# A hybrid decoder layer on one core: another order of the row phase, and half of the softmax normalisation on VectorE

## The reference

```python
hn = rmsnorm(h, g_attn_norm)
z = hn @ w_in                     # q: 8 heads of 64, k and v: 2 heads of 64, u: 4 groups of 128
q, k = rmsnorm per head           # gains g_q, g_k
logits = q k^T / 8 + bias[bucket(distance)]     # a window of 128 keys, blocks of 128 queries
m = max(max(logits), sink)
probs = exp(logits - m) / (sum(exp(logits - m)) + exp(sink - m))
a = probs @ v
pooled_g = trailing mean of u_g over 2, 4, 8, 16 tokens, minus u_g
m_g = (pooled_g @ w_pool_g) * pool_scale_g
h = h + concat(a, m) @ w_out
h = h + (silu(hn @ w_gate) * (hn @ w_up)) @ w_down
h = h + sigmoid(rmsnorm(h) @ w_ple_gate) * (p @ w_ple_proj)
```

## Time and profile before

| | us |
|---|---|
| median of 3 runs | 2166.16 |
| lowest, highest | 2163.57, 2167.04 |
| the profiled execution, whole | 2166.23 |
| its span, first to last instruction | 2164.3 |
| TensorE busy in the span | 2094.3 |
| VectorE busy | 1405.8 |
| ScalarE busy | 963.7 |
| GpSimd busy | 304.6 |

### The profile page before, as it was taken

How to read it: one execution, slowest core, us unless ns; L and a number is a source line. 1 busy time by engine, 2 the same in 40 slices (tenths; PEclk the granted TensorE clock), 3 DMA queues, 4 the chain that set the end, 5 groups by cost and what they waited for, 6 DMA issues and landing times.

```text
span 2164.3 us, 27230 instructions
## 1 busy us (share of the span) xinstructions
PE 2094.3 (97%) x10008; PEld 1746.6 (81%) x10008; DVE 1405.8 (65%) x1994; ACT 963.7 (45%) x1608; POOL 304.6 (14%) x448
## 2 busy tenths in 40 slices
PE   6999999999899999999999999999999999999998
PEld 5787877877777888888888888788888888888887
DVE  4566775776777556565588865685655656987653
ACT  3375575676664333333343354533333333333542
POOL 1423244152322000000000010000000000000100
PEclk9999999999999999999999999999999999999999
DMA  6431435433275232322572413842323236533143
GB/s 175 117 79 49 132 76 154 117 98 108 59 248 185 69 102 68 95 81 65 203 258 83 132 40 108 223 137 73 98 69 104 67 102 211 213 112 103 49 125 99
DMA packets 198879, 253.46 MB, mean 117 GB/s; under 512 B 14923, under 2 KB 128252, under 8 KB 197468
## 3 DMA queue, kind: packets, MB, share of 16 engines
q1 hardware_dynamic: 183888, 207.73, 32.7%
q0 software_dynamic: 12880, 42.51, 5.5%
q10 hardware_dynamic: 1980, 1.50, 0.3%
HBM read 201.88 MB, written 49.80 MB: 116 GB/s over the span
## 4 chain that ended last, share of the span: by engine, by line
PE 84%; DVE 5%; issue 4%; ACT 3%; DMA 3%; POOL 1%; SPq 0%; ACTq 0%; DVEq 0%; POOLq 0%
PE bank L2324 12%; PE bank L2328 12%; PE bank L2326 12%; PE bank L2030 7%; PE bank L2386 6%; PE bank L2387 6%; PE bank L2388 6%; PE bank L2032 6%; PE bank L2031 6%; PE bank L2056 1%; PE bank L2098 1%; ACT w_hi L872 1%; PE bank L2111 1%; DMA raw<-in_w_ple_gate 1%; PE bank L2047 1%
## 5 line engine op out<-in xcount | busy, mean ns | idle before, releaser
L2324 PE MATMUL bank<-a_hi,ring_hi 128*128 128x512 f32 x1232 | 482.3, 391 | 5.9 <-ACT u L1105 3.0
L2328 PE MATMUL bank<-a_hi,ring_lo 128*128 128x512 f32 x1232 | 481.2, 391 | 0.0
L2326 PE MATMUL bank<-a_lo,ring_hi 128*128 128x512 f32 x1232 | 481.1, 390 | 0.0
L2324 PEld LDWEIGHTS bank<-a_hi,ring_hi 128*128 128x128 f32 x1232 | 232.4, 189 | 55.4 <-ACT u L1105 3.9
L2326 PEld LDWEIGHTS bank<-a_lo,ring_hi 128*128 128x128 f32 x1232 | 232.4, 189 | 48.3
L2328 PEld LDWEIGHTS bank<-a_hi,ring_lo 128*128 128x128 f32 x1232 | 232.2, 188 | 48.4
L1348 DVE TENSOR_TENSOR w_lo<-raw,w_hi 128x1024 fp32r<-128x1024 f32 x112 | 147.5, 1317 | 175.3 <-ACT w_hi L872 174.7
L2386 PE MATMUL bank<-d_hi 128*128 128x512 f32 x616 | 240.8, 391 | 0.0
L2388 PE MATMUL bank<-d_hi,d_lo 128*128 128x512 f32 x616 | 239.8, 389 | 0.0
L2387 PE MATMUL bank<-d_lo,d_hi 128*128 128x512 f32 x616 | 239.7, 389 | 0.0
L1182 ACT ACTIVATE d_hi<-keep 128x1024 fp32r<-128x1024 f32 x132 | 139.8, 1060 | 201.5 <-PE bank L2388 184.5
(11 more groups left out here) (237 smaller groups left out, 4018.8 us busy)
## 6 DMA issues: line engine op xcount, KB each, us to landing
hidden_T<-hid POOLq DMA_DIRECT2D x88, 256.0 KB, 2.3
raws<-in_w_gate SPq DMA_DIRECT2D x84, 256.0 KB, 4.6
raws<-in_w_up SPq DMA_DIRECT2D x84, 256.0 KB, 5.3
raw<-in_w_in SPq DMA_DIRECT2D x80, 256.0 KB, 3.9
keep<-hidden_T SPq DMA_DIRECT2D x66, 256.0 KB, 3.8
raw<-in_w_out SPq DMA_DIRECT2D x64, 256.0 KB, 4.0
raw<-in_w_ple_gate SPq DMA_DIRECT2D x64, 256.0 KB, 4.1
keep<-in_w_down SPq DMA_DIRECT2D x44, 256.0 KB, 4.2
```

The source lines that it names most:

```text
L2324: mm(dst[:, :], wh[:, g, cols], a_hi[o][:, k, :], start=fresh and k == 0, stop=False, skip_group_check=True)
L2326: mm(dst[:, :], wh[:, g, cols], a_lo[o][:, k, :], start=False, stop=False, skip_group_check=True)
L2328: ins = mm(dst[:, :], wl[:, g, cols], a_hi[o][:, k, :], start=False, stop=k == 3, skip_group_check=True)
```

## The change

1. **Dense hosting.** In z1, out2 and now the beginning of out0 and out3, steps stand one to a half. Before, four halves carried two steps (half 19 of z1, and halves 5, 8 and 11 of out2).
2. **Panels of the output projection** in the order 2, 3, 0, 1 (`OUT_ORDER`): pooled channels first, attention's channels last.
3. **Pooling earlier.** Its sums, mean and rest two steps earlier. `pool_y` of tiles 0 to 2 moves from the out section into halves 16 to 18 of the z section ahead of it, in `bank0` and `bank1`. For tile 3 it moves to halves 13 to 15 of out2 and half 0 of out3, ahead of the hosted step there.
4. **Late splits on VectorE.** In an even half that hosts a step, `w_lo` is made behind the step and not ahead of it. ScalarE's `w_hi` stays ahead.
5. **Norms.** The norm-1 pieces of blocks 0 and 1 alternate between `bank7` and `bank4`. The squares of the norm-2 rows move to halves 0 to 2, their scaling to halves 3, 6, 8 and 12, and one transposed piece from half 8 to half 10.
6. **Start.** The first two `norm_hi`/`norm_lo` come around the first `split`; every later one follows one block sooner; `load_constants` moves behind them, and VectorE's work on the constants moves into half 1 of z0.
7. **Normalisation.** ScalarE normalises the first head of each unit alone; VectorE normalises the second directly behind its reciprocal (a new `tensor_scalar` of 128 x 256). TensorE's transpose waits for both.

```diff
+DENSE_Z = {h: (h - 2,) for h in range(2, 20)}
+DENSE_O = {h: (h,) for h in range(16)}
+HOST = {("z", 1): ((0, DENSE_Z),), ("o", 0): ((0, {0: (18,)}), (1, SPREAD)), ("z", 2): ((1, SPREAD_Z),),
+        ("o", 1): ((2, SPREAD),), ("z", 3): ((2, SPREAD_Z),), ("o", 2): ((3, DENSE_O),),
+        ("o", 3): ((3, {h: (h + 16,) for h in range(3)}),)}
+OUT_ORDER = (2, 3, 0, 1)
...
+POOL_Z, POOL_Z_COPY = {16: (0,), 17: (1,), 18: (2, 3)}, {17: (0,), 18: (1,), 19: (2, 3)}
+POOL_O2, POOL_O2_COPY = {13: (0,), 14: (1,), 15: (2,)}, {14: (0,), 15: (1,)}
+POOL_O3, POOL_O3_COPY = {0: (3,)}, {0: (2,), 1: (3,)}
...
             def normalise(n, c):
                 act.wait_ge(rden_done, n + 1)
-                for j in range(2):
-                    ins = nc.scalar.activation(scores[:, c, j, 0:2 * P], scores[:, c, j, 0:2 * P], ACT.Copy,
-                                               scale=rden[:, c % 2, j:j + 1])
-                ins.then_inc(pnorm, 1)
+                nc.scalar.activation(scores[:, c, 0, 0:2 * P], scores[:, c, 0, 0:2 * P], ACT.Copy,
+                                     scale=rden[:, c % 2, 0:1]).then_inc(pnorm, 1)
...
                 nc.vector.reciprocal(rden[:, i, :], row_sum[:, i, :]).then_inc(rden_done, 1)
+                dve.wait_ge(rden_done, n + 1)
+                nc.vector.tensor_scalar(out=scores[:, c, 1, 0:2 * P], in0=scores[:, c, 1, 0:2 * P],
+                                        scalar1=rden[:, i, 1:2], scalar2=None, op0=ALU.mult
+                                        ).then_inc(pnorm2, 1)
...
                 pe.wait_ge(pnorm, n + 1)
+                pe.wait_ge(pnorm2, n + 1)
...
-                    if half % 2 == 0:
+                    late = bool(hosted_steps("z", t, half))
+                    if half % 2 == 0 and not late:
                         split(Z_AT[t] + half // 2 + 1)
...
                     hosted("z", t, half)
+                    if half % 2 == 0 and late:
+                        split(Z_AT[t] + half // 2 + 1)
...
                 if b == 1:
+                    norm_hi(0, bank[4], wide_hi, 0, 0)
                     split(0)
-                    load_constants()
+                    norm_hi(1, bank[5], wide_hi, 1, 0)
...
+            load_constants()
             z_section(0)
```

More of the change, by code:

```diff
@@ L323, in mix_of, with hosted_steps, pool_bank, norm1_bank @@
             return (wide_hi, wide_lo) if s == NT - 1 else (mix_hi, mix_lo)
+        def hosted_steps(kind, t, half):
+            return [(s, k) for s, steps in HOST.get((kind, t), ()) for k in steps.get(half, ())]
+        def pool_bank(s, g):
+            return bank[7 if s == NT - 1 else g % 2]
+        def norm1_bank(b, e):
+            return bank[4 if e and b < 2 else 7]
         def h_of(t):
@@ L742, in hosted @@
             def hosted(kind, t, half):
[L743 to L746 removed]
+                for s, k in hosted_steps(kind, t, half):
+                    attention_step(s, k)
             def store_n2(t, b, e):
@@ L761, in z_section @@
                 for half in range(20):
-                    if t >= 2 and 1 <= half <= 4:
-                        powers(NORM2[t - 2], half - 1)
+                    if t >= 2:
+                        for b in N2_SQUARES_AT.get(half, ()):
+                            powers(NORM2[t - 2], b)
                     if t in (0, 3):
@@ L999, in hosted @@
                     stage_q(s, 0)
-                if (kind, t) in HOST:
-                    s, steps = HOST[kind, t]
-                    for k in steps.get(half, ()):
-                        attention_step(s, k)
+                for s, k in hosted_steps(kind, t, half):
+                    attention_step(s, k)
             def z_section(t):
@@ L1930, in out_section @@
                 for half in range(16):
-                    if half % 2 == 0 and OUT_AT[t] + half // 2 + 1 < ROW_PANELS:
+                    due = half % 2 == 0 and OUT_AT[t] + half // 2 + 1 < ROW_PANELS
+                    late = bool(hosted_steps("o", t, half))
+                    if due and not late:
                         split(OUT_AT[t] + half // 2 + 1)
-                    if half < 4:
-                        pool_y_rest(t, half)
+                    for g in {2: POOL_O2_COPY, 3: POOL_O3_COPY}.get(t, {}).get(half, ()):
+                        pool_y_rest(3, g)
                     if t < 2:
@@ L1964, in out_section @@
                     hosted("o", t, half)
+                    if due and late:
+                        split(OUT_AT[t] + half // 2 + 1)
             dve.wait_ge(gain_landed, 16)
@@ L2143, in put_off @@
                     kind, t, half = ("o", t - 2, 16) if kind == "z" else ("z", t + 1, 20)
-                if (kind, t) in HOST:
-                    s, steps = HOST[kind, t]
-                    for k in steps.get(half - 1, ()):
-                        if next_block(k):
-                            return lambda: transpose_probs(s, k)
+                for s, k in hosted_steps(kind, t, half - 1):
+                    if next_block(k):
+                        return lambda: transpose_probs(s, k)
                 return None
@@ L2258, in out_section @@
                         pe.wait_ge(y_lo, 4 * t + 2 * r - 2)
-                    rows_half(at + c, part, xh, xl, (2 * r, 2 * r + 1),
-                              (0, 1, 2, 3), r == 0, r == 3, outp, free,
-                              behind_first=put_off("o", t, half))
-                    if half < 4:
-                        if half == 0 and t == 0:
-                            pe.wait_ge(wp_lo_done, 1)
-                        pool_y(t, half)
+                    rows_half(at + c, part, xh, xl, (2 * r, 2 * r + 1), (0, 1, 2, 3), first, last, outp,
+                              behind_first=put_off("o", t, half), before=free)
+                    for g in {2: POOL_O2, 3: POOL_O3}.get(t, {}).get(half, ()):
+                        pool_y(3, g)
                     if t < 2 and half in N1_AT:
```

181 lines of the change are left out of this document (96 added, 85 removed).

## The result

| | before | after |
|---|---|---|
| median, us (7 runs each) | 2166.23 | 2153.44 |
| lowest, highest | 2161.32, 2170.74 | 2146.24, 2156.39 |
| profiled execution, its span | 2164.3 | 2149.8 |
| TensorE idle in the span | 70.0 | 57.6 |

The ratio of the times is 0.9937, with a 95% interval of 0.9920 to 0.9953: 13.6 us faster, between 10 and 17. The forecast was 26.5 us faster. The sign held, and 2153.4 lies in the wide range of 2128 to 2156, but outside the band of 2134 to 2149 to which I gave 0.62; the size is half of what I gave. The result lies where one of the rivals put it ("the old waits come back", 2154). One execution of all that follow, the traced one of the run with the scaling later, took 4261 us and is left out of that run's median.

What follows compares the result with a forecast made beforehand. TensorE was taken as the bound, busy 2094.3 us of a 2164.3 us span, 70.0 idle. Terms: 31.5 + 4.0 - 9.0 = 26.5 us gained, giving 2139.5 us; band 2134 to 2149 (chance 0.62), wide range 2128 to 2156.

Steps and rivals of the forecast that it cites:

- the old waits come back: Rival on the row phase: half of the 30.6 and of the 3.4 us return, time 2154; chance 0.17.
- The old waits: Dense hosting, late splits, panel order, norms: TensorE's listed waits, 30.6 us, go; 2.5 us return elsewhere.
- Behind them nothing else is late by more than a step: Behind the removed waits, any other lateness is covered by 12 matmuls between two steps, some 2.8 us.
- The clock: Without waits over 2 us TensorE's clock stays up, 3.4 us gained; tile 3's new waits lose 1.7 us.
- The start: Kernel start: first projection near 14.5 us, second restart at 26 to 27; 4.0 us gained, bounds 1.4 and 4.6.
- The bound by `wp_raw`'s landing: At the start: load lands 12.4 us after issue, third panel some 2.5 us late, leaving 1.4 us gained.
- Pooling product of tiles 0 to 2: Moved behind the hosted step where banks 0 and 1 are free; costed at nothing.
- Pooling product of tile 3: Ahead of the hosted step in out2 and out3: new waits 3.3, 1.9, 2.1 us, plus 1.7 us of clock.
- The new instruction: VectorE's 64 `tensor_scalar` of the normalisation, 0.35 us each, fit in a 1.10 us wait; cost TensorE nothing.
- waits for GpSimd: Rival: each new `tensor_scalar` may wait 1.25 us for a GpSimd operation; at all 64 steps, 2171.7 us; slower, chance 0.04.
- The feed-forward phase: After the row phase: claimed to start with the same waits as before, with no term in the sum.

Runs made afterwards that it cites:

- The experiment: Changed kernel with tile 3's four pooling products issued on TensorE behind the hosted step, not ahead of it: 2145.1 us, 0.9912 of the kernel before.

## Why the prediction was right in sign and half in size

By the sign that I had set for being wrong, TensorE's waits between 40 and 640 us staying over 20 us, the account was wrong: they are 29.0 us. That the time still fell into the wide range is in part luck, for the start brought 1.0 us more than its term and the feed-forward phase 3.2 us that no term foresaw; without these 4.2 us the time would have been some 2157.6.

**The old waits (30.6 us, of which 2.5 were to return).** The step that failed is "Behind them nothing else is late by more than a step", with the 12 matmuls that were to cover it. I leave out what both kernels have (the waits at the end of z0 and the start of z1 and the one at out3's last panel, 5.8 us before and 5.5 after) and the pooling product. The rest of the waits between 40 and 637 us went from 31.1 us to 17.2, not to 2.5. 8.2 us of the 17.2 are waits for `w_lo`, 1.8 `kT_lo`, 2.1 `v_lo`, 1.8 `transpose_k`. I had costed the late splits only by what they free and gave no price to what they put last. The order itself showed it: in four halves `qk_normalise` stands ahead of `w_lo`. The run with `w_lo` ahead of the step shows that the late place itself was right, and worth more than I had it: 18 us.

**Average against stretch.** I argued with VectorE's 22.2 us free in 73 us, 1.1 us a step after the change. In the changed kernel z1's steps have next to no waits, as forecast. But z2 and z3 carry norm-2 scalings, `copy_kv` and GpSimd's levels in the same halves, and between 259 and 267.5 us VectorE has nothing free. z1's average said nothing of z2. My own rival had named it ("dense steps leave VectorE 1.1 us a step on average"); its place was z2 and z3, not out2, its mechanism the row's length.

**The clock (3.4 us gained, 1.7 lost again).** It brought nothing. The mean granted clock is 0.993 in the twelve executions of the changed kernel and in the forty of the kernel before alike. In the two profiles, between 40 and 600, it even went the other way, 3.4 us lost before and 6.8 after (5.1 in its second profile). The old slow stretches at 194 and 556 us are gone, as said. New ones stand behind the new waits at 416 and 567 us (two), and one behind a wait of 1.99 us at 91 us that both kernels have and that before left the clock up. Of the low clock after, 0.6 us of loss falls into waits and costs nothing. The premise that the clock stays up without waits over 2 us did not hold even before: there four waits of 2.06 to 2.64 us, at 280, 431, 519 and 543 us, had no low clock behind them.

**The start (4.0).** Right in both places: first projection at 14.54 for 14.5 forecast, second restart at 25.53 for 26.2. The gain is 4.9 and 5.0 us, a little over my upper bound of 4.6. The bound by `wp_raw`'s landing did not apply.

**Pooling product of tiles 0 to 2 (nothing).** Right: no wait at L2195 but tile 3's.

**Pooling product of tile 3 (7.3 us and 1.7 of clock).** Right: 3.08, 1.30 and 1.84 for 3.3, 1.9 and 2.1, together 6.2; the clock cost twice as much behind the first. The experiment removed it by the cause I had named.

**The new instruction (nothing).** The term was too small: by the run with both heads on ScalarE the part cost some 2 to 4 us, and 4 to 7 with the clock. In the trace 0.35 us, the value I took: 41 of the 64 have no GpSimd operation beside them, and each of these takes 0.35 or 0.36. Ten take over 0.5 us, and the mean of all is 0.44. Two of them, one in z2 and one in z1, with what stands beside each:

```profile
290.39 1.57 DVE L1502 TENSOR_SCALAR scores<-scores,rden 128x256 f32<-128x256 f32 x1
290.49 1.31 POOL L739 TENSOR_TENSOR mix_lo<-sums,mix_hi 128x512 fp32r<-128x512 f32 x1
152.78 1.15 DVE L1502 TENSOR_SCALAR scores<-scores,rden 128x256 f32<-128x256 f32 x1
152.49 1.29 POOL L739 TENSOR_TENSOR mix_lo<-sums,mix_hi 128x512 fp32r<-128x512 f32 x1 [1.91 <-ACT mix_hi L986]
```

All ten end within 0.2 us of the end of a GpSimd operation. The mechanism of the "waits for GpSimd" rival exists, in one instruction of six and not in all, and that it fits into the 1.1 us before `probsT_lo` can hold in z1 and not where VectorE's row is full. Which of these places make up the cost is not shown.

**The feed-forward phase ("starts with the same waits").** Not quite: before, TensorE waited 2.10 us at 688 us for ScalarE, and after it no longer does; with the clock behind it this phase is 3.2 us shorter in the profile (11.3 us are won by its first product, 14.5 at the end). I have no experiment on it.

The sum as measured in the two profiles: 13.9 (old waits, for 28.1) less 6.2 (for 7.3) less about 3.4 of clock (for a gain of 1.7), 5.0 (for 4.0) and 3.2 (for nothing) is 12.5, against 14.5 between the spans. Of the difference 0.6 us is low clock that ran out during waits; the rest stays open. Dense hosting, the panels' order, the norms and the pooling of tiles 0 to 2 were not run alone, so how the 13.9 us divide among them is not shown.

## What to carry to other kernels

When an instruction is moved behind a block of work, price the whole block, conflicts with other engines included, at each place where it now stands, and not the average slack of the best section; the order of the instructions gives the places. Where an engine's row has no gap up to the moment that the consumer waits for, reordering inside the row only renames the wait, and taking work out of it pays us for us. Test each part of a bundle on its own: here one part (the split normalisation) cost some us, 4 to 7 by the times, inside a change that won 13, and one place (`w_lo` late) carried more than the whole gain.
